# RWKV preparation stage: token mixing and small sums on GpSimd, early hats, and key sums behind the third G product

## The chip, the cores and the metric

One Trainium2 chip (trn2), one of its cores. The metric is the device time of one launch in microseconds. Engines in the profile's names: PE is TensorE (PEld its weight loads), DVE VectorE, ACT ScalarE, POOL GpSimd, SP SyncE, which here only issues DMAs.

## The reference, cut to what matters

A hybrid diffusion block (depth 1, 2048 latent tokens and 256 context tokens, width 1024): a normalised, modulated input goes through one projection into four mixers (gMLP, neighbourhood attention, bidirectional RWKV-7, pooling), which are gated, merged and projected. The edited stage is the part of the RWKV branch that needs no state yet:

```python
zf = centred_shift_mix(z_in, mu)      # z + (0.5 * (prev + next) - z) * mu, 7 tiles of 128 channels
r, k, v, w_lo, a_lo = split(zf)
kk = k * rw_kk;  kk = kk / max(sqrt(sum(kk * kk)), 1e-12)
for d in range(2):                    # forward, backward
    w = -softplus(-(w0[d] + tanh(w_lo) @ w2[d])) - 0.5
    a = sigmoid(a0[d] + a_lo @ a2[d])
    kd = k * (1 + (a - 1) * k_a)
    y[d] = wkv7_scan(r, exp(-exp(w)), kd, v, -kk, kk * a)
    bonus[d] = sum(r * kd * r_k) * v
o = groupnorm(y[0] + y[1]) + bonus[0] + bonus[1]
```

The scan is computed in chunks of 64 tokens. Per chunk this stage makes P and Q (what the chunk does to the state), G (what the state adds to the output) and Y (the part of the output inside the chunk); a later stage chains the states.

## The kernel before, in words

Three stages follow one another, with all engines meeting between them: the front stage (projection), `recurrence_stage` and `late_stages`. Inside the second, `recurrence_local_stage` is edited. It walks 2304 tokens in nine blocks of 256 (`RB`); each block n has two units, (n,0) forward and (n,1) backward. In every unit TensorE does the main work of this unit and, between it, the small products that prepare the next one. `nxt` is the unit prepared: (n,1) during (n,0), (n+1,0) during (n,1).

Each engine has its own instruction stream written out by hand; the order in it is the order of execution. Semaphores count results: `Turns` gives each named result of an engine a number within a unit (`U` numbers per unit), `done` raises the semaphore and `after(engine, unit, name)` waits for it.

TensorE's main work inverts a unit triangular 64x64 matrix per chunk and head in levels v = 1 to 5. Level v: product G{v}, evicted by VectorE with a mask (L1211); product X{v}, evicted by ScalarE (L1334); product Z{v}, evicted by ScalarE. X{v} waits for G{v}'s eviction, G{v+1} for that of X{v}. `beside(v)` is set between G{v} and X{v}: the SK product (v=1), the LoRA product for the decay "tw" and the turned b (2), the LoRA product for the rate "ta" and the turned k (3), the key sums "ks" (4), MV and the norm columns "rnT" (5). `between(v)` is set between Z{v} and G{v+1}: V (3), A (4). After level 5 follow the bonus product, W, the next unit's first scores SB (they wait for the hat b, L1152), the products of G and Y, the first inverse SM, and P and Q.

VectorE in a unit: the five G evictions; behind the first the P and Q of the unit before (`last_products`, L1203, L1204) and the mask product MK (L1220), which TensorE's "tw" group waits for; in (n,1) the seven mixes of block n+1 (L1099) and kk_sq (L1103); behind the third the decay (L1108 to L1113, a scan among them); behind the fourth the Newton steps for the norm (L1119 to L1125, only in (n,1)), kd (L1129) and in (n,0) the two kd_sum steps (L1133, L1134); behind the fifth the hats: kk, R (L1144), kka (L1147), A (L1148), K (L1150), B (L1152). ScalarE evicts, does tanh, the scalings of the seven tiles (L1280), the rates, and the exponentials "EI", "EN" and "tot" (L1311 to L1315), which the hats wait for. GpSimd makes the neighbour sums of a block (L1007), the first Z (L1049), copies R (L1051), resets the identities X0 and MB (L1056, L1064) and copies the LoRA weights of one direction into the buffer used by the products (L1061), once "ta" is done. SP loads z two blocks ahead (`load`, L964) and stores G, Y and the bonus.

Of the kernel before, what the change touches and what calls it, by code (L numbers as in the profile page):

```python
# [21 lines left out]
P = 128  # L22
# [8 lines left out]
CH = 64  # L31
# [800 lines left out]
class Turns:  # L832

    def __init__(self, ctx, nc, name, results, each=None, first=0, leaves_out=((), ())):
# [36 lines left out]
def recurrence_local_stage(nc, t, s, chain):  # L871
# [8 lines left out]
    with ExitStack() as ctx:  # L880
# [29 lines left out]
        lora, lora_of = sb("lora", [P, 2 * P]), sb("lora_both", [P, 2, 2 * P])  # L910
# [7 lines left out]
        U = 64  # L918
        mixes, newton = [f"{j}" for j in (6, 2, 3, 0, 1, 4, 5)], ["nx", "n0"] + [f"n{i}{x}" for i in range(3) for x in "abc"] + ["rx"]
        block_v = [f"mix{j}" for j in mixes] + ["ksq"] + newton + ["kk"]  # L920
        block_a = [f"scaled{j}" for j in mixes] + ["th", "kkr0", "kkr1", "rrk0", "rrk1"]
        prep_v = Turns(ctx, nc, "prep_vector", [f"mix{j}" for j in mixes] + ["ksq", "lw", "L", "Lx", "inc"] + newton
                       + ["kd", "kds", "bt", "kk", "R", "kka", "A", "K", "B", "bonus"], U,
                       leaves_out=(("Lx", "inc", "kds", "bt", "bonus"), block_v))
        prep_a = Turns(ctx, nc, "prep_scalar", [f"scaled{j}" for j in mixes]
                       + ["th", "kkr0", "kkr1", "tw0", "tw1", "rrk0", "rrk1", "ta0", "ta1", "u0", "u1", "EI", "EN", "tot"], U,
                       leaves_out=((), block_a))
        main_v = Turns(ctx, nc, "main_vector", ["G1.", "P0.", "Q0.", "P1.", "Q1.", "MK.", "G2.", "G3.", "G4.", "G5.", "Ya0.", "Gs0.", "Ya1.", "Gs1."],
                       U, first=1, leaves_out=(("Ya0.", "Ya1."), ()))
        main_a = Turns(ctx, nc, "main_scalar", ["X1.", "Z1.", "X2.", "Z2.", "Bt.", "X3.", "Z3.", "Kt.", "V.", "X4.", "Z4.", "At.", "MV.", "Z5.",  # L930
                                                "W0.", "W1.", "Y0.", "Y1."], U, first=1, leaves_out=((), ("V.", "Y0.", "Y1.")))
        main_g = Turns(ctx, nc, "main_pool", ["Z.", "R.", "X0.", "lora.", "MB."], U, first=1)
# [5 lines left out]
        nbr_set, pe_go, dve_go, kept_set, centre_set = (sem(n) for n in ("neighbours_set", "pe_go", "dve_go", "kept_identities_set", "centre_set"))  # L938
        pool_go, lora_set = sem("pool_go"), sem("first_lora_set")
# [18 lines left out]
        def _(sp):  # L958
            def load(n):
                if not first_block(n):  # L960
                    sp.wait_ge(nbr_set, n)
                    prep_a.after(sp, (n - 1, 0), "scaled5")
                c0 = 0 if first_block(n) else n * RB + 1
                sp.dma_start(zin[:], t["zT"][T_RW:T_RG, :, bass.ds(c0, RB + 2)].rearrange("k p t -> p k t")).then_inc(z_in, 16)  # L964

            load(0)
            for d in range(2):
                sp.dma_start(lora_of[0:CH, d, :], t["rw_w2"][0, d, :, :]).then_inc(consts_in, 16)
                sp.dma_start(lora_of[CH:P, d, :], t["rw_a2"][0, d, :, :]).then_inc(consts_in, 16)
# [17 lines left out]
            load(1)  # L987
            sp.wait_ge(rpb_in, 16)
# [6 lines left out]
            turn(NBLK - 1, False)  # L995
            sp.wait_ge(g_stored, 16 * 2 * NBLK)
# [5 lines left out]
        def _(pool):  # L1002
            def neighbours(n):
                pool.wait_ge(z_in, n * 16 + 16)
                if not first_block(n):
                    prep_v.after(pool, (n - 1, 0), "mix5")
                nc.gpsimd.tensor_tensor(nbr[:], zin[:, :, 0:RB], zin[:, :, 2:RB + 2], ALU.add).then_inc(nbr_set, 1)  # L1007

            def prologue():
# [15 lines left out]
                neighbours(0)  # L1025
                for v, b in enumerate(LEVELS):
# [12 lines left out]
                pool.wait_ge(consts_in, 16 * 12)  # L1039
                nc.gpsimd.tensor_copy(lora[:], lora_of[:, 0, :]).then_inc(lora_set, 1)  # L1040
                prep_p.after(pool, (0, 0), "ta")
                nc.gpsimd.tensor_copy(lora[:], lora_of[:, 1, :]).then_inc(main_g.sem, main_g.each)
# [3 lines left out]
            def unit(n, d, nxt):  # L1046
                tiled = lambda a: a.rearrange("p q g m t -> p (q g m) t")
                head_v.after(pool, (n, d), "MB.")
                main_g.done(nc.gpsimd.tensor_tensor(tiled(Z[:]), tiled(MB[:]), eight(lev0[:, d, :]), ALU.mult), d, "Z.")  # L1049
                pool.sem_inc(pool_go, 1)  # L1050
                main_g.done(nc.gpsimd.tensor_copy(Rk[:, d], AR[:, 1]), d, "R.")  # L1051
# [8 lines left out]
                pool.sem_inc(pool_go, 1)  # L1060
# [1997 lines left out]
```

## Time and profile before

| what | value |
|---|---|
| median of 3 runs | 2461.0 us (2460.78 to 2463.07) |
| the profiled execution, own time | 2462.29 us |
| its span | 2460.6 us |
| busy share of the span: PE, DVE, ACT, POOL | 92%, 63%, 41%, 11% |
| the edited stage within the span | about 1262 to 1792 us |
| mean granted TensorE clock | 0.969 |

In the timeline each row is one run of like instructions: start, time from the first start to the last end, engine, line, operation, out<-in, count, and in brackets the idle time of the engine before it and what released it. In the rows by group the time before the bar is busy time and mean duration, behind it idle time and releasers. A window's row gives the busy time and (count) for PE, PEld, DVE, ACT, POOL, then the granted TensorE clock, the DMA share and GB/s.

### The profile page before, as it was taken

What the parts mean: (1) busy time and instruction counts of PE and PEld (TensorE: products, weight loads), DVE (VectorE), ACT (ScalarE), POOL (GpSimd) and SP (SyncE); (2) the same over time, 40 slices, a digit from 0 to 9 for tenths busy, and PEclk for the clock granted to TensorE, in tenths of its full rate; (3) what the DMA queues carried; (4) which work ended last, traced back from release to release, by engine and by line L of the source; (5) the groups of instructions that cost most, each with busy time, mean ns of one, the idle gap of its engine ahead of it and who ended that gap; (6) DMA issues with size and microseconds to landing.
All of it is one profiled execution on the core that took longest, in us unless ns stands there. A gap on an engine that the chain in (4) does not pass through costs nothing. (4 is left out here: it accounts for less than half of the span.)

```text
span 2460.6 us, 66375 instructions
## 1 busy us (share of the span) xinstructions
PE 2263.6 (92%) x26630; PEld 1853.4 (75%) x26630; DVE 1551.8 (63%) x2611; ACT 1009.5 (41%) x1734; POOL 265.3 (11%) x335
## 2 busy tenths in 40 slices
PE   4999999999899999999947899999788799899998
PEld 2788878888688887888836777777657576688887
DVE  5756566666865456665635777777456676856754
ACT  5444234544532123445424555555333666411111
POOL 0000000000000000000031222222124663000000
PEclk7999999999999999999978999999978899999999
DMA  7344333333242333333330111110068523834542
GB/s 240 107 135 125 111 94 111 113 117 102 94 129 93 96 108 97 106 111 119 107 101 25 32 41 32 32 56 17 19 214 305 126 94 95 288 115 171 197 152 88
DMA packets 250306, 277.75 MB, mean 113 GB/s; under 512 B 30683, under 2 KB 174171, under 8 KB 247643
## 3 DMA queue, kind: packets, MB, share of 16 engines
q1 hardware_dynamic: 245306, 266.95, 33.9%
q10 hardware_dynamic: 4576, 8.40, 0.9%
q8 instruction: 70, 1.15, 0.2%
q0 software_dynamic: 320, 0.98, 0.2%
q14 instruction: 34, 0.27, 0.0%
HBM read 184.66 MB, written 91.62 MB: 112 GB/s over the span
## 5 line engine op out<-in xcount | busy, mean ns | idle before, releaser
L715 PE MATMUL proj_ps<-h_hi,w_hi 128*128 128x512 f32 x1656 | 649.5, 392 | 27.6 <-DVE h_lo L465 19.7
L716 PE MATMUL proj_ps<-h_lo,w_hi 128*128 128x512 f32 x1656 | 647.0, 391 | 0.0
L717 PE MATMUL proj_ps<-h_hi,w_lo 128*128 128x512 f32 x1656 | 646.4, 390 | 0.0
L318 ACT CAST w_hi<-w_raw 128x512 fp32r<-128x512 f32 x420 | 255.1, 621 | 694.0 <-PE proj_ps L717 353.2
L715 PEld LDWEIGHTS proj_ps<-h_hi,w_hi 128*128 128x128 f32 x1656 | 312.3, 189 | 98.2 <-issue 26.1
L717 PEld LDWEIGHTS proj_ps<-h_hi,w_lo 128*128 128x128 f32 x1656 | 312.2, 189 | 65.6
L716 PEld LDWEIGHTS proj_ps<-h_lo,w_hi 128*128 128x128 f32 x1656 | 312.4, 189 | 62.9
L482 DVE TENSOR_TENSOR w_lo<-w_raw,w_hi 128x512 fp32r<-128x512 f32 x420 | 283.2, 689 | 44.3 <-ACT w_hi L318 43.7
L498 DVE TENSOR_TENSOR z_slots<-proj_ps,x_rows 128x512 f32<-128x512 f32 x174 | 120.2, 691 | 169.9 <-PE proj_ps L717 167.9
L498 DVE TENSOR_TENSOR x_rows<-proj_ps,x_rows 128x512 f32<-128x512 f32 x116 | 80.1, 691 | 108.9 <-PE proj_ps L717 102.9
L1010 POOL MEMSET rpb_padded<- 60x127 f32 x1 | 0.2, 198 | 1261.3 <-POOLq L89 1261.3
L1211 DVE TENSOR_TENSOR inv_g<-rw_ps,level_masks 128x512 f32<-128x512 f32 x90 | 62.1, 690 | 97.2 <-PE rw_ps L1387 97.1
L2903 PE MATMUL late_ps<-late_lo,mw_hi 128*128 128x512 f32 x252 | 98.0, 389 | 0.0
L1334 ACT COPY inv<-rw_ps 128x512 f32<-128x512 f32 x72 | 42.0, 583 | 125.0 <-PE rw_ps L1387 125.0
L494 DVE COPY x_rows<-proj_ps 128x512 f32<-128x512 f32 x58 | 40.0, 690 | 73.6 <-PE proj_ps L717 73.5
L2492 DVE CUSTOM_DVE_ANT_0 scores<-na_ps,bias_windows 128x768 f32<-128x768 f32 x64 | 61.3, 957 | 34.4 <-issue 25.3
L2448 ACT ACTIVATE late_rows<-scores,softmax_stats 128x768 f32<-128x768 f32 x64 | 60.1, 940 | 52.3 <-DVE softmax_stats L2495 52.3
L2945 PE MATMUL late_ps<-wo_hi,y_hi 128*128 128x512 f32 x208 | 81.3, 391 | 0.0
L2947 PE MATMUL late_ps<-wo_hi,y_lo 128*128 128x512 f32 x208 | 81.0, 389 | 0.0
L2946 PE MATMUL late_ps<-wo_lo,y_hi 128*128 128x512 f32 x208 | 80.9, 389 | 0.0
L332 ACT ACTIVATE z_slots<-z_slots 128x512 f32<-128x512 f32 x128 | 70.6, 621 | 14.1 <-DVE z_slots L498 9.0
L2728 ACT ACTIVATE late_ps<-late_rows 128x1024 f32<-128x1024 f32 x15 | 15.4, 1030 | 125.8 <-DVE late_rows L2818 125.8
(380 smaller groups left out, 4101.4 us busy)
## 6 DMA issues: line engine op xcount, KB each, us to landing
w_raw<-in_w_in SPq DMA_DIRECT2D x240, 256.0 KB, 3.0
scratch_gatesT<-z_slots SPq DMA_DIRECT2D x128, 256.0 KB, 2.7
late_rows<-scratch_gatesT SPq DMA_DIRECT2D x64, 512.0 KB, 4.4
scratch_zT<-z_slots SPq DMA_DIRECT2D x108, 256.0 KB, 2.4
ada<-in_ada_w SPq DMA_DIRECT2D x4, 2048.0 KB, 15.2
late_rows<-scratch_zT SPq DMA_DIRECT2D x4, 2048.0 KB, 12.7
late_rows<-scratch_branchT SPq DMA_DIRECT2D x16, 512.0 KB, 5.3
late_rows<-in_x SPq DMA_DIRECT2D x16, 512.0 KB, 4.9
```

The source lines that it names most:

```text
L318: A.copy(wh[:, i, :, :], raw[:, q, :, :]).then_inc(w_hi, 1)
L332: A.activation(zs[:, q, :], zs[:, q, :], ACT.Sigmoid).then_inc(gated, 1)
L482: V.tensor_tensor(wl[:, i, :, :], raw[:, W_SOURCE[i], :, :], wh[:, i, :, :].bitcast(F32), ALU.subtract).then_inc(w_lo, 1)
L498: V.tensor_tensor(to, ps[:, BANK[n], :], part[:, {1: 0, 3: 0, 4: 2, 5: 0, 6: 1}[n], :], ALU.add).then_inc(ev, 1)
L715: T.matmul(out, wh[:, i, k, :], hi[:, o, k, :], start=(first and k == 0), stop=False, skip_group_check=not first)
L716: T.matmul(out, wh[:, i, k, :], lo[:, o, k, :], start=False, stop=False, skip_group_check=not first)
L717: last = T.matmul(out, wl[:, i, k, :], hi[:, o, k, :], start=False, stop=(k == 3), skip_group_check=not first)
L1211: done(V.tensor_tensor(eights(G[:]), ps[:, 2:4, 0:256].rearrange("p q (k t) -> p q k t", t=CH), mask, ALU.mult), f"G{v}.", *(("P0.", "Q0." ...
L2903: T.matmul(o, hi, b_lo[:, i % 2, k, :], start=False, stop=False)
L2945: T.matmul(o, y_hi[:, k, rows], wo_hi[:, k, cols], start=(k == 0), stop=False)
L2946: T.matmul(o, y_hi[:, k, rows], wo_lo[:, k, cols], start=False, stop=False)
L2947: last = T.matmul(o, y_lo[:, k, rows], wo_hi[:, k, cols], start=False, stop=(k == KT - 1))
```

## The change

Work moves from VectorE and ScalarE to GpSimd, several steps of the next unit's preparation come earlier, and buffers change:

- The mix of a block is made on GpSimd alone, block-wide: neighbour sums, times mu/2, own values times 1 - mu (in place in the loaded tile), then sums "z6", "z23", "z01", "z45". kk_sq, kd_sum and its product with r_rk, the identity added to P, and Y forward plus Y backward go to GpSimd as well. ScalarE copies P and the backward unit's Y out of PSUM for that.
- The LoRA weights of a direction are loaded by SP into the one buffer `lora` for each unit, after "ta"; GpSimd's copy goes. The load of z for block n+2 stands behind this in SP's queue.
- The key sums follow the third G product, and the norm squares (nx) are evicted behind the third G eviction.
- R, K (and kka in the backward case) are made behind the fourth G eviction by `hats_early`, which waits for "tot"; `hats`, behind the fifth, keeps kk, kka of the forward case, B and A, in this order. The exponentials come before the w_in copy in (n,0) and before the X4 copy in (n,1). tanh and the raw keys of the next block are made at the end of (n,0).

The diff, cut to its core (the prologue's counterparts, names of semaphores and buffers are left out):

```diff
 # SP
             def turn(n, more):
                 for d in range(2):
+                    if not (last and d):
+                        prep_p.after(sp, (n + d, 1 - d), "ta")
+                        load_lora(d)
+                    if d == 0 and not first_block(n):
+                        y_out(n - 1)
                     if d and more:
                         load(n + 2)
                     main_v.after(sp, (n, d), "Gs1.")
...
+            def y_out(n):
+                sp.wait_ge(y_added, n + 1)
+                sp.dma_start(t["yT"]..., yst[:]).then_inc(y_stored, 16)
 # GpSimd
+            def scaled_neighbours(n):
+                pool.wait_ge(mix_step, n * 3 + 1)
+                G_.tensor_tensor(nbr[:], nbr[:], per_tile(hmu), ALU.mult).then_inc(mix_step, 1)
+            def scaled_own(n):
+                pool.wait_ge(mix_step, n * 3 + 2)
+                G_.tensor_tensor(own, own, per_tile(omu), ALU.mult).then_inc(mix_step, 1)
+            def mixed_tiles(n, name, j, k):
+                mix_g.done(G_.tensor_tensor(zf[:, j:k, :], nbr[:, j:k, :], own[:, j:k, :], ALU.add), 0, name)
+            def bonus_rows(n):
+                prep_v.after(pool, (n, 1), "kd")
+                keys_g.done(G_.tensor_tensor(kds[:], kd[:, 0], kd[:, 1], ALU.add), 1, "kds")
+                keys_g.after(pool, (n, 1), "kds")
+                prep_a.after(pool, (n, 0), "rrk1")
+                keys_g.done(G_.tensor_tensor(kds[:], kds[:], rrk[:], ALU.mult), 1, "bt")
...
             def unit(n, d, nxt):
                 head_v.after(pool, (n, d), "MB.")
                 main_g.done(... Z ..., d, "Z.")
+                if d and nxt:
+                    key_squares(n + 1)
+                    mixed_tiles(n + 1, "z01", 0, 2)
+                    prep_v.after(pool, (n, 1), "bonus")
+                    mixed_tiles(n + 1, "z45", 4, 6)
                 kept = nc.gpsimd.tensor_copy(Rk[:, d], AR[:, 1])
+                    main_a.after(pool, before, "P.")
+                    main_g.done(add_identity(*before), d, "P.")
+                    if d == 0:
+                        add_y(n - 1)
                 main_p.after(pool, (n, d), "G1.")
                 main_g.done(... X0 ..., d, "X0.")
-                if d == 0 and not (isinstance(n, int) and n == NBLK - 1):
-                    neighbours(n + 1)
-                prep_p.after(pool, nxt, "ta")
-                main_g.done(nc.gpsimd.tensor_copy(lora[:], lora_of[:, d, :]), d, "lora.")
+                if d == 0:
+                    if more:
+                        scaled_own(n + 1)
+                        prep_p.after(pool, nxt, "ta")
+                        mixed_tiles(n + 1, "z6", 6, 7)
+                    bonus_rows(n)
+                    if more:
+                        mixed_tiles(n + 1, "z23", 2, 4)
+                elif not (isinstance(n, int) and n >= NBLK - 2):
+                    neighbours(n + 2)
+                    scaled_neighbours(n + 2)
                 main_p.after(pool, (n, d), "G5.")
                 main_g.done(... MB ..., d, "MB.")
...
 # VectorE
             def last_products(n, d, done):
-                main_p.after(dve, (n, d), "PQ.")
+                main_a.after(dve, (n, d), "P.")
-                    done(V.tensor_tensor(to(Pst), pq[:, :, 0, :, :], eye, ALU.add), f"P{c}.")
...
                     if v == 3 and nxt:
+                        if d:
+                            norm_squares(nxt[0])
                         decay(*nxt)
                     if v == 4 and nxt:
                         if d:
                             norms(nxt[0])
                         rates(*nxt)
-                        if d == 0:
-                            bonus_rows(n)
+                        hats_early(*nxt)
                 if nxt:
                     hats(*nxt)
 # ScalarE, unit
-                if nxt and d:
-                    scaled(nxt[0])
-                    tanh_lo(nxt[0])
                 factor(X[:], "X1.", 4)
...
                 if nxt:
                     key_rates(*nxt)
+                    if d:
+                        exps(*nxt)
+                        bonus_keys(nxt[0])
                 factor(X[:], "X4.", 4)
                 factor(Z[:], "Z4.", 0)
+                if nxt and d == 0:
+                    exps(*nxt)
                 main_p.after(act, (n, d), "A.")
                 own(A.copy(... WI ...), "At.")
-                if nxt:
-                    exps(*nxt)
...
+                for c in range(2):
+                    own(A.copy((yst2 if d else yst)..., ...), f"Y{c}.")
+                if d == 0 and not (isinstance(n, int) and n == NBLK - 1):
+                    tanh_lo(n + 1)
+                    raw_keys(n + 1)
+                main_p.after(act, (n, d), "PQ.")
+                main_g.after(act, (n, d), "P.")
+                own(A.copy(pst[:], ...), "P.")
 # TensorE
                     if v == 2:
-                            main_g.after(pe, u, "lora.", 1)
+                            pe.wait_ge(lora_in, u + U)
                     if v == 3:
                         if more:
                             a_lora(u, -1)
+                            key_sums(u, -1)
                         main_a.after(pe, u, "Bt.")
                         turned(Kh, "K.")
-                    if v == 4 and more:
-                        key_sums(u, -1)
...
-                    if v == 4 and more:
+                    if v == 3 and more:
                         prep_v.after(pe, u, "nx", -1)
...
             def first_scores(u, back):
-                prep_v.after(pe, u, "B", back)
+                prep_v.after(pe, u, "A", back)
```

## Rows read from the trace of the kernel before

**Rows 1.** Windows, one block's units: us, busy PE, PEld, DVE, ACT, POOL, clock, DMA

```profile
1418.27:1443.53 25.26, 23.53 (x871) 20.20 (x871) 17.95 (x30) 14.30 (x31) 7.51 (x6) 1.00 0.06 21
1443.53:1470.35 26.82, 23.80 (x870) 20.33 (x871) 19.95 (x45) 15.17 (x33) 4.77 (x5) 1.00 0.17 54
```

**Rows 2.** Timeline of TensorE in (n,0): start, us, [idle before <- releaser]

```profile
1430.49 0.69 PE L1387 MATMUL rw_ps<-inv,m_b 64*64 64x64 f32 x32
...
1431.11 1.05 PE L1387 MATMUL rw_ps<-heads,kk_sq 128*128 128x2 f32 x8
...
1432.10 0.69 PE L1387 MATMUL rw_ps<-inv_g,inv_t 64*64 64x64 f32 x32
...
1435.27 0.69 PE L1387 MATMUL rw_ps<-inv_t,inv_g 64*64 64x64 f32 x32
...
1436.95 1.10 PE L1387 MATMUL rw_ps<-w_in_rows,inv_t 64*64 64x128 f32 x32
...
1438.92 1.10 PE L1387 MATMUL rw_ps<-a_r_hat,b_hat 64*64 64x128 f32 x32 [0.87 <-DVE b_hat L1152]
...
1439.82 0.44 PE L1387 MATMUL rw_ps<-m_r,w_rows 64*64 64x64 f32 x16
```

**Rows 3.** Timeline of TensorE in (n,1)

```profile
1448.18 0.69 PE L1387 MATMUL rw_ps<-inv,m_b 64*64 64x64 f32 x32 [0.61 <-ACT inv L1334]
...
1458.52 0.69 PE L1387 MATMUL rw_ps<-inv_g,inv_t 64*64 64x64 f32 x32 [0.44 <-DVE kk_norm_inv L1120]
...
1462.06 0.69 PE L1387 MATMUL rw_ps<-inv_t,inv_g 64*64 64x64 f32 x32 [0.31 <-issue]
```

**Rows 4.** Groups by line in the stage: busy us, mean ns | idle before, releaser

```profile
L1099 DVE SCALAR_TENSOR_TENSOR z_mixed<-neighbours,half_mu,z_mixed 128x256 f32<-128x256 f32 x63 | 26.9, 475 | 0.7 <-ACT z_mixed L1280 0.7
```

**Rows 5.** Timeline of ScalarE in (n,0)

```profile
1433.34 0.59 ACT L1334 COPY inv_t<-rw_ps 128x512 f32<-128x512 f32 x1
...
1435.34 0.21 ACT L1315 COPY chunk_decay<-e_padded 128x8 f32 x1
...
1438.12 1.07 ACT L1375 COPY w_rows<-rw_ps 128x512 f32<-128x512 f32 x2 [1.50 <-PE rw_ps L1387]
```

**Rows 6.** Timeline of VectorE in (n,0)

```profile
1432.20 0.69 DVE L1129 TENSOR_TENSOR k_d<-k_rate,z_mixed 128x512 f32<-128x512 f32 x1 [0.26 <-ACT k_rate L1305]
...
1434.41 0.69 DVE L1211 TENSOR_TENSOR inv_g<-rw_ps,level_masks 128x512 f32<-128x512 f32 x1
...
1435.68 0.69 DVE L1144 TENSOR_TENSOR a_r_hat<-z_mixed,e_padded 128x512 f32<-128x512 f32 x1 [0.58 <-ACT chunk_decay L1315]
...
1438.10 0.68 DVE L1152 SCALAR_TENSOR_TENSOR b_hat<-kk_a,e_neg 128x512 f32<-128x512 f32 x1
```

**Rows 7.** Timeline of VectorE in (n,1)

```profile
1453.83 1.23 DVE L1109 TENSOR_TENSOR_SCAN log_run<-scan_keep,log_w 128x512 f32<-128x512 f32 x1
...
1458.31 0.17 DVE L1120 TENSOR_SCALAR kk_norm_inv<-kk_norm_sq 128x8 int32<-128x8 int32 x1
...
1460.33 0.43 DVE L1125 COPY kk_norm_rows<-kk_norm_inv 128x512 f32<-128x512 f32 x1
```

**Rows 8.** Timeline of GpSimd: the prologue, then (n,1)

```profile
1268.64 3.17 POOL L1007 TENSOR_TENSOR neighbours<-z_halo 128x1792 f32<-128x1792 f32 x1 [1.60 <-DMA z_halo<-scratch_zT]
...
1453.87 1.38 POOL L1061 COPY lora<-lora_both 128x256 f32<-128x256 f32 x1 [8.41 <-PE rw_ps L1387]
```

**Rows 9.** Groups of GpSimd by line, the whole kernel: busy us, mean ns

```profile
L1049 POOL TENSOR_TENSOR inv_t<-m_b,level_turned 128x512 f32<-128x512 f32 x18 | 23.0, 1278 | 113.8 <-DVE m_b L1165 113.8
...
L2437 POOL TENSOR_TENSOR wo_rows<-wo_rows,late_rows 128x1024 f32<-128x1024 f32 x8 | 18.7, 2386 | 22.6 <-DMA wo_rows<-in_w_out 22.6
```

**Rows 10.** Timeline of VectorE in the stage's prologue

```profile
1271.25 0.59 DVE L1087 TENSOR_SCALAR one_less_mu<-mu 128x7 f32<-128x7 f32 x1 [5.71 <-DMA rw_params<-in_rw_a]
```

**Rows 11.** Timeline of SP's queue at the stage's end

```profile
1786.38 0.47 SPq L981 DMA_DIRECT2D scratch_yT<-y_stage  x1
```

**Rows 12.** DMA issues: KB each, median us to landing

```profile
z_halo<-scratch_zT SPq DMA_DIRECT2D x9, 903.0 KB, 5.2
```

More of the change, by code:

```diff
@@ L841, in __init__ @@
         for d in range(2):
-            ends = [self.at[r] - 1 for r in self.made[d][1:]] + [self.each + self.at[self.made[1 - d][0]] - 1]
+            if not self.made[d]:
+                self.adds.append({})
+                continue
+            first = self.each + self.at[self.made[1 - d][0]] if self.made[1 - d] else 2 * self.each + self.at[self.made[d][0]]
+            ends = [self.at[r] - 1 for r in self.made[d][1:]] + [first - 1]
             self.adds.append({r: e - self.at[r] + 1 for r, e in zip(self.made[d], ends)})
@@ L925, in recurrence_local_stage @@
[L925 to L929, printed above, removed]
+        U = 32
+        newton = ["nx", "n0"] + [f"n{i}{x}" for i in range(3) for x in "abc"] + ["rx"]
@@ L987, in _ @@
             load(1)
+            prep_p.after(sp, (0, 0), "ta")
+            load_lora(1)
             sp.wait_ge(rpb_in, 16)
@@ L1038, in prologue @@
                     masks.step(pool, nc.gpsimd.tensor_tensor(lev0[:, d, :], lev[:, 1 - d, 0, :], i64[:], ALU.add))
[L1039 to L1042, printed above, removed]
+                neighbours(1)
+                scaled_neighbours(1)
             eight = lambda m: m.rearrange("p (o t) -> p o t", o=1).to_broadcast([P, 8, CH])
@@ L1064, in unit @@
                 main_g.done(nc.gpsimd.tensor_copy(tiled(MB[:]), eight(i64[:, :])), d, "MB.")
-            units(pool, prologue, unit)
+            prologue()
+            unit(0, 0, (0, 1))
+            unit(0, 1, (1, 0))
+            with hinted_loop(nc, pool, 1, NBLK - 2) as n:
+                unit(n, 0, (n, 1))
+                unit(n, 1, (n + 1, 0))
+            unit(NBLK - 2, 0, (NBLK - 2, 1))
+            unit(NBLK - 2, 1, (NBLK - 1, 0))
+            unit(NBLK - 1, 0, (NBLK - 1, 1))
+            unit(NBLK - 1, 1, None)
+            main_a.after(pool, (NBLK - 1, 1), "P.")
+            add_identity(NBLK - 1, 1).then_inc(pool_go, 1)
+            add_y(NBLK - 1)
         N_MASKS = 1 + 8 * len(LEVELS) + 2 * 5 + 2
@@ L1129, in rates, with hats_early @@
                 prep_v.done(V.tensor_tensor(kd[:, d], uu[:], zf[:, 2:4, :], ALU.mult), d, "kd")
-            def bonus_rows(n):
-                prep_v.after(dve, (n, 1), "kd")
-                prep_v.own(dve, (n, 1), V.tensor_tensor(kds[:], kd[:, 0], kd[:, 1], ALU.add), "kds")
-                prep_v.done(V.tensor_tensor(kds[:], kds[:], rrk[:], ALU.mult), 1, "bt")
+            def hats_early(n, d):
+                done = lambda ins, name: prep_v.done(ins, d, name)
+                prep_a.after(dve, (n, d), "tot")
+                if not (first_block(n) and d == 0):
+                    main_g.after(dve, (n, d), "R.", back=1)
+                if d == 0:
+                    mix_g.after(dve, (n, 0), "z01")
+                done(V.tensor_tensor(chunks(AR[:, 1, :, :]), chunks(zf[:, 0:2, :]), padded(d, 1 - d), ALU.mult), "R")
+                prep_v.after(dve, (n, d), "kd")
+                done(V.tensor_tensor(Kh[:], kd[:, d], EN[:], ALU.mult), "K")
+                if d:
+                    done(V.scalar_tensor_tensor(kka[:], aa[:], 1.0, kk[:], ALU.add, ALU.mult), "kka")
             def hats(n, d):
@@ L1182, in prologue @@
                 rates(0, 0)
+                hats_early(0, 0)
                 hats(0, 0)
@@ L1272, in _ @@
             act.wait_ge(consts_set.sem, 8)
[L1274 to L1280 removed]
             def tanh_lo(n):
[L1283 removed]
+                mix_g.after(act, (n, 0), "z6")
                 prep_a.done(A.activation(th[:], zf[0:CH, 6, :], ACT.Tanh), 0, "th")
             def raw_keys(n):
[L1287 removed]
+                mix_g.after(act, (n, 0), "z23")
                 for p in range(2):
@@ L1318, in prologue @@
             def prologue():
-                scaled(0)
                 tanh_lo(0)
@@ L1412, in key_sums @@
             def key_sums(u, back):
-                prep_v.after(pe, u, "ksq", back)
+                mix_g.after(pe, u, "ksq", back)
                 for g in range(2):
```

166 lines of the change are left out of this document (81 added, 85 removed).

## The prediction

> **What bounds the kernel now.** I first split the span by stage. The edited stage prepares the RWKV recurrence, in nine blocks of two units each. The windows of one steady block show 25.26 us for the unit (n,0) and 26.82 for (n,1), 52.08 together. TensorE is busy 23.5 and 23.8 of these at a granted clock of 1.00, VectorE 18.0 and 20.0, GpSimd only 7.5 and 4.8 [rows 1]. So at most some 4.8 us per block, 43 us in all, can be won by taking waits away, and every microsecond by which a product is held up is paid in full. The timelines of TensorE, ScalarE and VectorE in one block show where it waits: 0.87 us for b_hat in each unit [rows 2], 0.61 for a ScalarE copy in (n,1) (it stands behind the tanh) and 0.44 for the first norm step [rows 3]. Elsewhere each eviction is covered by a product set beside it.
>
> **The change part by part.** Times below are those of the shown block, moved.
>
> *Work leaves VectorE and ScalarE.* The seven mixes (26.9 us in nine blocks [rows 4]) go, and ScalarE's seven scalings of the same tiles, with kk_sq, the two kd_sum steps, the identity added to P and the addition of Y. ScalarE gains a copy of P per unit and the Y copies of the backward unit, about 0.6 each like its other copies [rows 5], at the unit's end, where it idles. Of this relief only what stood before a waiting product counts: the mask product MK comes two steps earlier, 0.15 us for TensorE in (n,0); in (n,1) this and the tanh are worth 0.8.
>
> *Key sums.* G4 is issued at 1430.49, the key sums at 1431.11, X4 at 1432.10 [rows 2]. X4 needs G4's eviction: 0.69 product, 0.07, 0.69 VectorE [rows 6], 0.14, together 1.59 us, and 1.61 is there. The key sums (0.99) cost nothing now: they lie in that wait. After G3 there is already a LoRA product and a transpose, so there they are added in full, and behind G4 the wait stays, empty. Cost +0.99 in (n,0), less the 0.15 above: X4 moves to about 1432.9. In (n,1) X4 waited 0.44 more anyway [rows 3]; with the 0.8 won, X4 comes 0.4 earlier than now.
>
> *The early hats.* VectorE's R, K and kka now stand between G4's eviction and G5's, and the first waits for "tot" of ScalarE. In (n,0) ScalarE makes it after the Z4 copy. That copy moves from 1433.34 to about 1434.1. From it to tot were 2.00 us, to 1435.34, with a copy of 0.48 between that now comes after; tot takes 0.21 [rows 5]: it is there at 1435.87. VectorE's hats have a pitch of 0.605 (1435.68 to 1438.10 is four [rows 6]), so G5's eviction starts at 1435.94 + 1.81 = 1437.75, ends at 1438.4, and Z5 is issued at 1438.57, where it was 1435.27 [rows 2]: +3.3 us. (The w_in copy, now behind the exponentials, also holds the norm columns, but only to about 1436.4.) Given back: b_hat is now ready in time. The G/Y products waited for the scores behind b_hat (they start at 1439.82, 4.55 after Z5); now they wait for the copies of W: 1.68 from Z5 to W, 1.10, 0.07, 1.07, 0.15 [rows 2, 5] are 4.07. **(n,0) without any contention: +3.3 - 0.5 = +2.8.**
> In (n,1) the exponentials precede the X4 copy and with the r_rk copies delay it (G5 +0.7). VectorE has ten Newton steps (2.0 us, from 1458.31 to the spread at 1460.33 [rows 7]), the spread, kd, R and K before G5's eviction. They start 0.3 earlier, behind G4's eviction, but R and K come on top: Z5 about 1463.0 where it was 1462.06 [rows 3]; less 0.5: **+0.5**.
>
> *GpSimd.* Without the LoRA copies it keeps about 10 us per block (four small groups per unit) and gets: scaled neighbours, scaled own, the sums of 1792 columns, kk_sq, two kd_sum steps, four identity additions and the Y addition. The nearest rows: 3.17 for 1792 columns where both inputs are of one tensor (1.77 ns per column), 1.28 for 512 with a broadcast (2.5) and 2.39 for 1024 (2.3) where they are two [rows 8, 9]. I take 2.3, as these read two tensors: 4.2 us for each scaling, bounds 3.17 and 4.5. That makes about 29 us of 52: not a bound by itself.
>
> *VectorE against GpSimd.* What counts is when they meet. GpSimd's LoRA copy of 256 columns at 1453.87 took 1.38 us, more than twice a 512-column copy: VectorE's scan of two SBUF inputs ran 1453.83 to 1455.06, and the copy ended 0.2 after it [rows 7, 8]. The other way round: VectorE's 7-column one_less_mu started at 1271.25, took 0.59 and ended at 1271.84, 0.03 after GpSimd's neighbours (1268.64 + 3.17) [rows 8, 10]. So each waits for the other's whole instruction. Nowhere before does a VectorE step with two SBUF inputs start inside a long GpSimd one; I take it that it waits like the 7-column one; the other bound is that it doesn't wait at all.
> The Trainium skill (SBUF — State Buffer, "SBUF: two separate sides") states this as a rule: the pair of ports is locked for the whole instruction, also against VectorE operations with two SBUF inputs. By that rule the sum is the first one below, without it the second.
> (n,0): bt ends at about 1436.4 (kd, 0.69 from 1432.20 [rows 6], comes 0.9 later with the key rates, then two steps of 1.2), 0.5 after VectorE could start R; then z23 (1.2) and the identity copy (0.6) can slip in between R, K and kka. Z5 +0.5 to +2.5 more, I take 1.5: **+4.3**.
> (n,1): the load of z for block n+2 was issued at the unit's start; now it stands in SP's queue behind the wait for "ta" and two LoRA loads. The LoRA copy at 1453.87 waited for this same ta [rows 8]; it comes 0.9 earlier, plus three issues of 0.5 (like 0.47 [rows 11]) and 5.2 to landing [rows 12]: 1459.7. Then GpSimd adds (3.17) and scales (4.2) without a pause but for a semaphore, to about 1467.3: just where VectorE does the last Newton steps, the spread, kd, R and K. It gets one or two small steps in between; then kd, R, K (1.8) and possibly the identity copy, so G5's eviction ends at about 1470.0 and Z5 is issued at 1470.2, +8.2; less 0.5: **+7.7** (bounds +5.5 and +8.7). Seven blocks have such a load; the eighth such unit costs +0.5.
>
> *Ends of the stage.* Prologue: the LoRA product no longer waits for the masks, but GpSimd mixes block 0 before building them and runs block 1's neighbours before its first Z; -2 to +2, taken as 0, as G1 still needs the masks. End: Y was stored from 1786.38 [rows 11]; now it follows the P copy, two identity additions and the sum, issued near 1790.6: +4.5 at the barrier. LoRA loads of two 64 KB have a unit's time before their use: 0. The waits for y_added and y_stored lie a unit behind: 0.
>
> **Sum:** 9 x 4.3 + 7 x 7.7 + 0.5 + 4.5 = +98 us. The profiled execution took 2462.3 us (span 2460.6), 1.3 above the median of 2461.0; 2462.3 + 98 - 1.3 = 2559; rounded down for the smaller bounds, **2556 us**.
>
> **Rivals.**
> 1. *The engines don't exclude each other* in this pairing: 9 x 2.8 + 8 x 0.5 + 4.5 = +34, 2495 us. For it: the one VectorE wait on record is of a small one-input step. Against: the scan shows the opposite direction for just this form.
> 2. *The lock holds, but loads land beside other work* (z earlier or later than the Newton steps, VectorE's run not broken): half of (n,1)'s price, 9 x 3.5 + 7 x 3.5 + 5 = +61, 2522 us.
> 3. *Faster:* the relief of VectorE reaches TensorE. Place: G5's eviction. If tot and the three hats were done before G5's product ends, all waits of [rows 2, 3] go (0.87 twice, 0.44, 0.61, about 0.7 of small ones: 3.5) and only the key sums (1.4 per block) stay: 9 x -2.1 + 4.5 = -15, 2446 us. It decides where tot is 2.6 us earlier in (n,0) than I work out and GpSimd's long steps meet no VectorE step. Against: ScalarE's order is written out, Z4's copy before the exponentials.
> 4. *Nothing measurable:* gains and losses cancel; only by accident.
> The clock stays at 1.00 (2.4 GHz) in this stretch [rows 1]; longer idle times of TensorE might lower it, which the upper end allows for.
>
> **How the numbers follow.** Chances: forecast 0.5, rival 1 0.2, rival 2 0.15, faster 0.12, nothing 0.03. The forecast's own range is 2525 to 2590. The range over the cases, 2482 to 2590, leaves out the faster and the equal case and a little above. A difference of over 0.2% (5 us) can be told from none here; slower 0.85, same 0.03, faster 0.12.
>
> **What would show it.** Right: in (n,0) VectorE waits for tot before R, and G5's eviction follows kka; X4 is released by G4's eviction with no product between; in (n,1) GpSimd runs two long instructions back to back some 16 us into the unit while a VectorE step that took 0.2 or 0.68 us lasts several; the block period is near 64 us. No VectorE duration stretched and a period of 55 makes rival 1 right; GpSimd's long steps elsewhere, rival 2; a period under 52, rival 3.

## The result: slower by 4.7%, and the profile after

| | before | after |
|---|---|---|
| median of 4 runs each, us | 2462.0 (2460.8 to 2466.1) | 2579.9 (2572.6 to 2580.5) |
| ratio | | 1.047, 95% interval 1.045 to 1.049 |
| profiled execution, span, us | 2460.6 | 2577.9 |
| first G1 of the stage, us | 1310.41 | 1312.49 |
| last G1 of the stage, us | 1759.73 | 1878.32 |
| busy share PE, DVE, ACT, POOL | 92%, 63%, 41%, 11% | 89%, 60%, 39%, 16% |
| mean granted TensorE clock | 0.969 | 0.949 |

Predicted were 2556 us and a range of 2482 to 2590. All of the loss lies in the stage: from its first to its last G1 there are 565.8 us instead of 449.3, 116.5 more, and the spans differ by 117.3. The windows of one steady block, (n,0) and then (n,1), answer to [rows 1] (columns as there):

```profile
1448.34:1479.74 31.40, 24.91 (x871) 20.69 (x871) 17.45 (x24) 14.63 (x32) 14.47 (x12) 0.95 0.06 21
1479.74:1515.61 35.87, 26.78 (x871) 22.23 (x871) 22.34 (x34) 13.74 (x30) 14.62 (x12) 0.86 0.14 44
```

(n,0) is 6.1 us longer and (n,1) 9.1. GpSimd is busy 29 us of 67 and bounds nothing by itself, but TensorE's busy time rose by 1.4 and 3.0 us for the same number of products. The granted clock (0.95 and 0.86, the third number from the right) was 1.00 in both units before.

**(n,0).** TensorE, to hold against [rows 2] (start, us, and idle time before it with its releaser):

```profile
1461.39 0.69 PE L1455 MATMUL rw_ps<-inv,m_b 64*64 64x64 f32 x32
1462.94 0.69 PE L1455 MATMUL rw_ps<-inv_g,inv_t 64*64 64x64 f32 x32 [0.86 <-issue]
...
1466.63 0.63 PE L1494 MATMUL rw_ps<-ident,kk_norm_rows 128*128 128x128 f32 x4 [1.04 <-ACT w_in_rows L1430]
1470.57 1.13 PE L1455 MATMUL rw_ps<-inv_t,inv_g 64*64 64x64 f32 x32 [3.31 <-DVE inv_g L1295]
1471.63 2.06 PE L1455 MATMUL rw_ps<-kd_sum,heads 128*128 128x512 f32 x2
1473.62 1.10 PE L1455 MATMUL rw_ps<-w_in_rows,inv_t 64*64 64x128 f32 x32
...
1476.01 0.46 PE L1455 MATMUL rw_ps<-m_r,w_rows 64*64 64x64 f32 x16 [0.41 <-ACT w_rows L1436]
```

X4 (the row at 1462.94) has nothing between it and G4 and waits 0.86 us: the cover of the key sums is gone. Its row names "issue", but what came last was G4's eviction, which ended 0.10 us before it (1462.15 + 0.69, first row below). Z5 waits 3.31 us for G5's eviction. The wait for b_hat of [rows 2] is gone, as the scores follow the W product at once. VectorE and GpSimd in the same stretch show why the eviction is late:

```profile
1462.15 0.69 DVE L1295 TENSOR_TENSOR inv_g<-rw_ps,level_masks 128x512 f32<-128x512 f32 x1 [1.29 <-PE rw_ps L1455]
...
1466.03 1.20 DVE L1223 TENSOR_TENSOR a_r_hat<-z_mixed,e_padded 128x512 f32<-128x512 f32 x1 [2.23 <-ACT chunk_decay L1381]
1467.15 1.66 DVE L1225 TENSOR_TENSOR k_hat<-k_d,e_neg 128x512 f32<-128x512 f32 x1
1468.73 1.09 DVE L1227 SCALAR_TENSOR_TENSOR kk_a<-a_tanh,kk_unit 128x512 f32<-128x512 f32 x1
1469.75 0.68 DVE L1295 TENSOR_TENSOR inv_g<-rw_ps,level_masks 128x512 f32<-128x512 f32 x1
```
```profile
1465.41 1.27 POOL L1046 TENSOR_TENSOR kd_sum<-kd_sum,r_rk 128x512 f32<-128x512 f32 x1 [0.23 <-ACT e_padded L1377]
1466.63 1.63 POOL L1035 TENSOR_TENSOR z_mixed<-neighbours,z_halo 128x512 f32<-128x512 f32 x1
1468.21 1.07 POOL L1144 COPY m_b<-ident 128x512 f32<-128x512 f32 x1
```

R waits 2.23 us for tot and stands ahead of the eviction. Then the engines take turns: R, K and kka take 1.20, 1.66 and 1.09 us where one took 0.69 before [rows 6], each with a GpSimd step that ends inside it.

**(n,1).** The queue of SP, then GpSimd, VectorE and TensorE:

```profile
1489.22 0.48 SPq L969 DMA_DIRECT2D lora<-in_rw_w  x1
1489.74 0.60 SPq L970 DMA_DIRECT2D lora<-in_rw_a  x1
1490.64 0.41 SPq L966 DMA_DIRECT2D z_halo<-scratch_zT  x1
```
```profile
1495.86 3.17 POOL L1024 TENSOR_TENSOR neighbours<-z_halo 128x1792 f32<-128x1792 f32 x1 [10.45 <-DMA z_halo<-scratch_zT]
1499.11 3.19 POOL L1028 TENSOR_TENSOR neighbours<-neighbours,half_mu 128x1792 f32<-128x1792 f32 x1
```
```profile
1495.68 0.17 DVE L1207 TENSOR_TENSOR kk_norm_step<-kk_norm_inv,kk_norm_sq 128x8 f32<-128x8 f32 x1
1495.88 3.18 DVE L1208 SCALAR_TENSOR_TENSOR kk_norm_step<-kk_norm_step,kk_norm_inv 128x8 f32<-128x8 f32 x1
1499.09 0.17 DVE L1209 SCALAR_TENSOR_TENSOR kk_norm_inv<-kk_norm_step,kk_norm_inv 128x8 f32<-128x8 f32 x1
1499.29 3.29 DVE L1210 COPY kk_norm_rows<-kk_norm_inv 128x512 f32<-128x512 f32 x1
1502.50 1.09 DVE L1214 TENSOR_TENSOR k_d<-k_rate,z_mixed 128x512 f32<-128x512 f32 x1
...
1504.72 0.68 DVE L1295 TENSOR_TENSOR inv_g<-rw_ps,level_masks 128x512 f32<-128x512 f32 x1
```
```profile
1502.73 1.09 PE L1494 MATMUL rw_ps<-ident,kk_norm_rows 128*128 128x128 f32 x4 [4.99 <-DVE kk_norm_rows L1210]
1505.55 1.13 PE L1455 MATMUL rw_ps<-inv_t,inv_g 64*64 64x64 f32 x32 [1.73 <-DVE inv_g L1295]
1506.61 2.07 PE L1455 MATMUL rw_ps<-kd_sum,heads 128*128 128x512 f32 x2
1508.62 1.99 PE L1455 MATMUL rw_ps<-w_in_rows,inv_t 64*64 64x128 f32 x32
```

The z load lands 16.1 us into the unit. GpSimd's two long steps start at once, and an 8-column Newton step of VectorE that began 0.02 us after the first took 3.18 us instead of 0.17 and ended 0.03 after it; the spread, begun in the second, took 3.29 instead of 0.43 [rows 7]. TensorE waits 4.99 + 1.73 us.

**The clock.** The products behind both waits are slow: the bonus product took 2.06 and 2.07 us, against 1.12 in experiment 7 below, where the clock stays up. Windows of the two units, from Z5 to the start of the next unit's scores in (n,0), and to their end in (n,1):

```profile
1470.57:1474.55 3.98, 3.98 (x67) 2.37 (x70) 1.59 (x3) 0.59 (x1) 0.00 (x0) 0.63 0.00 0
1505.55:1511.89 6.34, 6.23 (x99) 4.40 (x99) 2.43 (x4) 1.66 (x3) 0.00 (x0) 0.56 0.00 0
```

The granted clock is 0.63 and 0.56 on average here, so for most of both windows it was at 0.5, the lower of its two levels (1.2 of 2.4 GHz). In (n,1) it was already at 0.50 from 1502.73 to 1505.55, between the two waits: there the norm columns took 1.09 us.

### The profile page after: what moved, and what is told of

It is laid out like the page before. It is cut to its first block and busy times, and to the rows that moved or that the text cites. A ratio compares the mean times of both kernels' runs of the same rounds, so it can differ in the third digit from the quotient of the medians.

```text
span 2577.9 us, 66380 instructions
## 1 busy us (share of the span) xinstructions
PE 2297.9 (89%) x26630; PEld 1874.2 (73%) x26630; DVE 1559.6 (60%) x2467; ACT 1000.7 (39%) x1707; POOL 417.1 (16%) x442
## 5 line engine op out<-in xcount | busy, mean ns | idle before, releaser
L715 PE MATMUL proj_ps<-h_hi,w_hi 128*128 128x512 f32 x1656 | 650.0, 392 | 28.6 <-DVE h_lo L465 20.9
L1455 PE MATMUL rw_ps<-inv_t,inv_g 64*64 64x64 f32 x2880 | 67.8, 234 | 40.5 <-DVE inv_g L1295 40.5
L1399 ACT COPY inv_t<-rw_ps 128x512 f32<-128x512 f32 x90 | 53.1, 590 | 101.6 <-PE rw_ps L1455 101.6
L1455 PEld LDWEIGHTS rw_ps<-inv_t,inv_g 64*64 64x64 f32 x2880 | 58.2, 148 | 45.2 <-issue 45.2
```

The costliest lines, as they stand in the source:

```text
L715: T.matmul(out, wh[:, i, k, :], hi[:, o, k, :], start=(first and k == 0), stop=False, skip_group_check=not first)
L1399: own(A.copy(to.rearrange("p q g m t -> p q (g m t)"), ps[:, bank:bank + 2, 0:256]), name)
L1455: mm = lambda o, l, r, start=True, stop=True: T.matmul(o, l, r, start=start, stop=stop)
```

## The experiments

A ratio is to runs of the kernel before on the same chip; "units" are distances from G1 to G1 in steady blocks. Before: (n,0) 25.3, (n,1) 26.8, together 52.1. After: 31.4 to 32.4 and 34.9 to 35.9, together 66.5 to 68.0.

**1. After, with the z load ahead of the LoRA loads.**

```diff
+                    if d and more:
+                        load(n + 2)
                     if not (last and d):
                         prep_p.after(sp, (n + d, 1 - d), "ta")
                         load_lora(d)
...
-                    if d and more:
-                        load(n + 2)
```

> The changed kernel with the load of z for block n+2 put ahead of the wait for ta and of the two LoRA loads on SP. Theory (the two long GpSimd instructions shut VectorE out during the Newton steps): they then run about 8 to 16 us into the unit (n,1), where VectorE mostly evicts PSUM; the unit falls from 35.9 us to 29 to 31, and TensorE's clock no longer drops behind it; in all 35 to 48 us less, 2532 to 2545. Rival (VectorE's own chain in (n,1) is simply too long, or the clock drops by itself): under 5 us less, above 2575.

Measured: 2537.3 us, 1.029 (1.027 to 1.031). (n,1) fell to 29.8, (n,0) stayed at 31.7. GpSimd starts 8.3 us into the unit instead of 16.1, and the same two GpSimd steps now meet other VectorE steps, the Newton steps none:

```profile
1479.39 1.20 DVE L1190 TENSOR_SCALAR log_w<-log_w 128x512 f32<-128x512 f32 x1
1480.70 4.01 DVE L1191 TENSOR_TENSOR_SCAN log_run<-scan_keep,log_w 128x512 f32<-128x512 f32 x1
1484.83 0.69 DVE L1295 TENSOR_TENSOR inv_g<-rw_ps,level_masks 128x512 f32<-128x512 f32 x1
```

The scan took 4.01 us instead of 1.23 [rows 7], and X4 waits 2.9 us for the eviction behind it. So the load's place costs 43 us, and GpSimd's steps hold VectorE where they fall now too, only at a cheaper place.

**2. After, with R, K and kka behind the fifth eviction.** The call of `hats_early` moves to where `hats` is called.

```diff
                         rates(*nxt)
-                        hats_early(*nxt)
                 if nxt:
+                    hats_early(*nxt)
                     hats(*nxt)
```

> The changed kernel with the early hats (R, K, kka) called behind the fifth G eviction, as before the change. Theory (R to kka hold the fifth eviction and with it Z5): the unit (n,0) falls from 31.4 to 27 to 28.5 us; in (n,1) only R and K move, while the long GpSimd instructions still hold kd, so it falls by 1 to 2.5; in all 40 to 50 us less, 2530 to 2540. Rival (order on VectorE does not matter, GpSimd's instructions set the pace): under 10 us less.

Measured: 2533.4 us, 1.028 (1.026 to 1.030); (n,0) 27.6 at a clock of 1.00, (n,1) 33.8 at 0.90. The early hats cost 4 to 5 us in (n,0), the clock's fall behind their wait included. In (n,1) two Newton steps took 3.04 and 3.03 us: the collision is untouched.

**3. After, with the key sums behind G4.** The call and the first norm step go back to where they were.

```diff
                             a_lora(u, -1)
-                            key_sums(u, -1)
...
+                    if v == 4 and more:
+                        key_sums(u, -1)
```

> The changed kernel with the key sums and the norm squares back behind the fourth G product. Theory (behind G3 they are added in full, behind G4 they fill a wait that is there anyway): 0.9 us less in (n,0), 0.5 to 0.9 in (n,1), 12 to 16 us less in all, about 2566. Rival (their place is free): within 3 us of 2580.

Measured: 2569.1 us, 1.041 (1.039 to 1.043); two units about 66. The direction is right; the size is known to some microseconds only, as the runs spread from 2561 to 2577.

**4. Before, with the key sums behind G3 and nothing else** (the same edit the other way, on the kernel before).

> The kernel before with this one part of the change: key sums and norm squares behind the third G product. Theory: +1.0 us in (n,0), +0.5 in (n,1), 12 to 15 us more, about 2475. Rival: they come earlier and free the 0.44 us wait for the norm, so no loss or a gain of up to 4 us (2458 to 2462).

Measured: 2476.9 us, 1.0046 (1.0031 to 1.0061). (n,0) 26.1, (n,1) 27.15: +0.85 and +0.33, where the prediction has 0.99, and in (n,1) 0.99 less the 0.44 that X4 waited anyway. X4 waits 0.86 in both units.
That is five of the eight (n,1) units. The other three took 28.6 us, at a clock of 0.94. In the one that starts at 1448.04, the clock is 0.54 from 1460 to 1463 us, and the V product behind Z3 took 1.62 us instead of 1.16. No wait of TensorE above 0.86 us stands in that unit, and none above 0.61 ahead of the fall: here the clock fell without a long stall.

**5. Before, with R, K and kka ahead of the fifth eviction.** Of the rest of the change it has only what belongs to this order: `hats` makes B ahead of A, and the scores wait for A.

```diff
                         if d == 0:
                             bonus_rows(n)
+                        hats_early(*nxt)
                 if nxt:
                     hats(*nxt)
```

> The kernel before with one part of the change alone: VectorE makes R hat, K hat and (in the backward unit) kka ahead of the eviction of G5. Mixing stays on VectorE, key sums behind G4, z load where it was. Theory (the hats hold G5's eviction until tot and three steps of 0.605 us are done, with no contention from GpSimd): (n,0) longer by 1.5 to 2.5 us, (n,1) by 0 to 0.5, so some 54.5 to 55 for two units instead of 52.1, about 2482 to 2490 us in all, and Z5 waits some 3 us for the eviction in (n,0). Rival (the order of the hats costs nothing by itself, it is GpSimd that makes the wait): within 3 us of before, about 2462 to 2465.

Measured: 2508.9 us, 1.018 (1.017 to 1.020): more than expected. The windows of four units of this kernel, two (n,0) and two (n,1), say where the rest comes from:

```profile
1398.66:1428.56 29.90, 25.39 (x870) 21.16 (x871) 20.16 (x45) 15.12 (x33) 4.76 (x5) 0.94 0.16 48
...
1428.56:1456.43 27.87, 23.59 (x871) 20.23 (x871) 17.95 (x30) 14.39 (x31) 7.50 (x6) 1.00 0.06 19
1486.21:1516.28 30.07, 26.27 (x870) 22.12 (x871) 17.97 (x30) 14.32 (x31) 7.52 (x6) 0.89 0.05 17
...
1516.28:1544.55 28.27, 23.90 (x870) 20.30 (x871) 20.18 (x45) 15.19 (x33) 4.77 (x5) 1.00 0.17 51
```

At a clock of 1.00 the order alone costs +2.6 us in (n,0) (27.87) and +1.45 in (n,1) (28.27). The same unit of the same program takes 1.6 to 2.2 us more when the clock fell in it (29.90, 30.07), with TensorE's busy time up by 1.5 and 2.7. That happened in about half of the units, behind a wait of 2.3 to 2.9 us for the eviction; the same wait is also there in units where the clock held, so it does not follow from the wait's length alone. (TensorE's rows name "issue" for this wait; in (1,0) the eviction ended at 1390.70 and Z5 followed at 1390.80.)

**6. After with all three undone.** The handing to GpSimd stays, and with it the exponentials' new place and A behind B.

> The kernel after with three parts undone together: z load ahead of the LoRA loads in SP's queue, the hats behind G5's eviction, the key sums behind G4. What is left is the handing of mixing and sums to GpSimd. Theory (the three costs are separate, and what remains of the loss is GpSimd's long steps meeting VectorE elsewhere): (n,0) about 26.5 to 27, (n,1) 28 to 29, 55 for two units, 2485 to 2500 us, still slower than before. Rival (once the order is right, VectorE's relief of three mixes per unit pays): two units under 52, below 2460 us. Second rival (the parts overlap, so undoing the third gives nothing more): like the better of the two single undoings less 30 us, above 2503 us.

Measured: 2494.5 us, 1.012 (1.011 to 1.014). (n,0) 26.74, (n,1) 29.4 to 29.8. VectorE in (n,1), and GpSimd's two steps:

```profile
1465.62 0.69 DVE L1295 TENSOR_TENSOR inv_g<-rw_ps,level_masks 128x512 f32<-128x512 f32 x1 [3.07 <-PE rw_ps L1454]
1466.22 2.74 DVE L1190 TENSOR_SCALAR log_w<-log_w 128x512 f32<-128x512 f32 x1
1469.07 4.01 DVE L1191 TENSOR_TENSOR_SCAN log_run<-scan_keep,log_w 128x512 f32<-128x512 f32 x1
```
```profile
1465.51 3.17 POOL L1024 TENSOR_TENSOR neighbours<-z_halo 128x1792 f32<-128x1792 f32 x1 [2.75 <-DMA z_halo<-scratch_zT]
1468.76 3.24 POOL L1028 TENSOR_TENSOR neighbours<-neighbours,half_mu 128x1792 f32<-128x1792 f32 x1
```

The eviction, which reads PSUM and one mask, ran its 0.69 us inside GpSimd's step. The two steps behind it, SBUF only, did not: 2.74 and 4.01 us instead of 0.42 and 1.22. X4 waits 3.2 us for what VectorE does behind them (2.6 in the first block), and in all seven of these units the clock falls (0.94 over the unit). In the (n,1) units of experiment 1, with a wait of 2.6 to 3.0 us at the same place, it stayed at 1.00. The one (n,1) unit without a load took 26.31, half a microsecond under before: the only place where relieving VectorE of the mixes shows as a gain. (n,0) is 1.5 over: R, K and kka still take 1.04, 1.67 and 1.09 us there, and TensorE waits 1.2 for A hat behind them. What is left of the change loses 30 us, the clock's part in it included.

**7. The kernel of experiment 1 with idle time filled.** Four products from constants ahead of the wait for G5's eviction; the result is read by nobody.

```diff
+                    if v == 5:
+                        for _ in range(4):
+                            mm(ps[:, 0, 0:256], J[:], tri[:].rearrange("p a b c -> p (a b c)"))
                     main_v.after(pe, u, f"G{v}.")
```

> The kernel of a1 (after with the early z load, 2537 us) with four products of 128x256 columns from constants set between the norm columns and Z5, about 2.1 us of TensorE work whose result nobody reads. They lie in the wait for G5's eviction, 3.31 us in (n,0) and 1.68 us in (n,1). Theory (TensorE's clock falls to its lower level because it idled in (n,0), and the bonus product and W behind the wait then take 2.02 and 1.83 us instead of 1.13 and 1.10): with the wait filled the clock stays at 1.00 there, (n,0) is 1.3 to 1.7 us shorter, (n,1) 0.4 longer where the products overshoot, 2525 to 2531 us. Rival (the clock falls for another reason, or its fall costs nothing in time): the two products as slow as before, 2537 to 2542 us.

Measured: 2524.3 us, 1.024 (1.023 to 1.026), 13 us less with more work for TensorE. TensorE in (n,0), first in experiment 1, then filled:

```profile
1459.31 0.69 PE L1455 MATMUL rw_ps<-inv_t,inv_g 64*64 64x64 f32 x32 [3.31 <-DVE inv_g L1295]
1459.93 2.02 PE L1455 MATMUL rw_ps<-kd_sum,heads 128*128 128x512 f32 x2
1461.88 1.83 PE L1455 MATMUL rw_ps<-w_in_rows,inv_t 64*64 64x128 f32 x32
```
```profile
1457.26 1.89 PE L1455 MATMUL rw_ps<-chunk_masks,heads 128*128 128x256 f32 x8
1460.74 0.69 PE L1455 MATMUL rw_ps<-inv_t,inv_g 64*64 64x64 f32 x32 [1.59 <-DVE inv_g L1295]
1461.36 1.12 PE L1455 MATMUL rw_ps<-kd_sum,heads 128*128 128x512 f32 x2
1462.42 1.10 PE L1455 MATMUL rw_ps<-w_in_rows,inv_t 64*64 64x128 f32 x32
```

(n,0) went from 31.7 to 30.0 at a clock of 1.00, and the two products run at full speed; so they do in all seven units from (1,0) to (7,0), none of which kept the clock in experiment 1. (n,1) is 29.4 to 31.1: there the clock now falls in six of the seven units with a load, around X4's wait; in experiment 1 it fell in none of them, with that wait at 2.6 to 3.0 us. So the time behind the stall in (n,0) is a cost of its own, and TensorE's idling there is what brings it on; where else the clock falls, these runs do not say.

**8. After, with GpSimd's two long steps writing only.** This kernel leaves out the neighbours of blocks 2 to 8; all other work stands where it was.

```diff
-                    neighbours(n + 2)
-                    scaled_neighbours(n + 2)
+                    for k in range(2):
+...
+                        G_.tensor_tensor(nbr[:, :, 0:1], zin[:, :, 0:1], zin[:, :, 2:3], ALU.add)
+                        G_.memset(nbr[:, :, 1:RB], 0.5).then_inc(mix_step, 1)
```

> The kernel after, where GpSimd's two long steps in (n,1) are replaced, in the loop and in the units around it, by a 7-column addition (it carries the wait) and a fill of the same 1785 columns with a constant. So the neighbours of blocks 2 to 8 are not computed; everything else stands, the place of the steps too. Theory (GpSimd shuts VectorE out because both read SBUF at the same pair of ports, so it counts what the two instructions read): the fills, which read nothing, either do not hold VectorE at all or only for their own, shorter, time; then (n,1) falls from 35.9 to about 27.7, what the unit without a load took in after, and the total to about 2520 us (7 blocks of 8). Rival (any GpSimd instruction shuts VectorE out for its whole length): Newton steps of VectorE last as long as a fill, and (n,1) is longer than 27.7 by the two fills' durations, 2525 to 2550 us according to their length.

Measured: 2533.9 us, 1.028 (1.027 to 1.030). GpSimd, then VectorE:

```profile
1483.65 1.59 POOL L1147 MEMSET neighbours<- 128x1785 f32 x1
...
1485.52 1.58 POOL L1147 MEMSET neighbours<- 128x1785 f32 x1
```
```profile
1483.77 0.17 DVE L1214 SCALAR_TENSOR_TENSOR kk_norm_step<-kk_norm_step,kk_norm_inv 128x8 f32<-128x8 f32 x1
1483.97 0.17 DVE L1215 SCALAR_TENSOR_TENSOR kk_norm_inv<-kk_norm_step,kk_norm_inv 128x8 f32<-128x8 f32 x1
1484.17 1.35 DVE L1216 COPY kk_norm_rows<-kk_norm_inv 128x512 f32<-128x512 f32 x1
...
1486.04 0.68 DVE L1229 TENSOR_TENSOR a_r_hat<-z_mixed,e_padded 128x512 f32<-128x512 f32 x1
```

Neither theory holds as put. The steps with two SBUF inputs run through both fills at their usual 0.17 and 0.68 us; only the spread, a copy with one input, was held (1.35 instead of 0.43). (n,1) took 28.2 and 28.4 in the two units where the clock stayed at 1.00, near the 27.7 expected, and 29.9 to 30.0 in the five where it fell. The total missed its 2520 by 14 us; those falls, 1.6 us each, are 8 of them.
The Trainium skill (SBUF — State Buffer, "SBUF: two separate sides") says that VectorE steps with two SBUF inputs are excluded only against a GpSimd step that reads SBUF, and those in a two-port mode against any. It names a copy of fp32 within SBUF as such a step, which the spread is. The trace agrees on both counts: 0.17 and 0.68 us beside the fill, 1.35 for the copy.

**9. Before, with K hat behind B hat.** A version to beat both.

```diff
                 prep_v.after(dve, (n, d), "kka")
                 done(V.scalar_tensor_tensor(Bh[:], kka[:], 0.5, EN[:], ALU.mult, ALU.mult), "B")
+                prep_v.after(dve, (n, d), "kd")
+                done(V.tensor_tensor(Kh[:], kd[:, d], EN[:], ALU.mult), "K")
```

> The kernel before with VectorE's K hat moved behind B hat, nothing else. B hat is what TensorE waits for (0.87 us in each unit), K hat is needed only behind G1 of the next unit. Theory (that wait ends last in the unit): each of 18 units shorter by one VectorE step of about 0.5 to 0.6 us, 8 to 10 us in all, 2452 to 2454 us, and the wait for b_hat is 0.3 us. Rival (the G/Y products wait for the copies of W right behind, and cover the wait): 2461 to 2463 us.

Measured: 2456.4 us, 0.9963 (0.9949 to 0.9976). Units 24.79 and 26.33, each 0.48 shorter. The wait for b_hat is 0.27 us where it was 0.87 [rows 2].

**10. The kernel of 9 with ScalarE's tanh behind the X1 copy.**

```diff
                     scaled(nxt[0])
-                    tanh_lo(nxt[0])
                 factor(X[:], "X1.", 4)
+                if nxt and d:
+                    tanh_lo(nxt[0])
```

> The kernel of b3 (before with K hat last, 2456 us, units 24.79 and 26.33) with ScalarE's tanh of the next block set behind the copy of X1 instead of ahead of it in (n,1). Theory (G2 waits 0.61 us there for the copy, which stands behind a tanh that waits for VectorE's mix of tile 6): (n,1) shorter by 0.3 to 0.6 us, eight times, so 2451 to 2454 us, ratio to before about 0.994. Rival (the LoRA product behind G2 then waits for the tanh, or the copy of Z1 comes late): (n,1) 26.2 to 26.4, 2455 to 2458 us.

Measured: 2456.8 us, 0.9960 (0.9944 to 0.9975). (n,1) is 26.06, 0.27 shorter: the wait of 0.61 for the X1 copy is gone, and 0.47 for the mask product MK took its place ahead of the LoRA product. Eight times 0.27 is 2.2 us, which the runs cannot tell from experiment 9. Both beat the kernel before.

## Why the prediction was right, and which terms were off

**What held.** The sign, the place and both mechanisms: in (n,0) VectorE waits for tot ahead of R with G5's eviction behind kka; X4 has nothing to cover its wait; in (n,1) GpSimd's long steps run back to back 16 us into the unit and a step of 0.17 us lasts 3.2. Only the block period, forecast near 64 us, was 66.5 to 68. Rival 1 (no exclusion) fell with these rows. Rival 2 (the load lands beside other work) was made true by experiment 1, which gave 2537 us and not the 2522 of its price: even there the steps met the scan. The faster rival fell by experiment 6: VectorE's relief shows as 0.5 us in the one (n,1) unit that GpSimd's long steps don't disturb.

**Term by term**, for the steady block shown:

| term | predicted | measured |
|---|---|---|
| (n,0): Z5 later in the unit | +4.8 | +5.2 (22.23 instead of 17.00 behind G1) |
| (n,1): Z5 later in the unit | +8.2 | +7.3 (25.81 instead of 18.53) |
| b_hat given back, each unit | -0.5 | -0.5 at a clock of 1.00 (7.79 from Z5 to the next G1 in the (n,1) unit without a load, 8.29 before) |
| from Z5 to the next G1, (n,0) | 7.8 | 9.2 |
| from Z5 to the next G1, (n,1) | 7.8 | 10.1 |
| unit (n,0) | +4.3 | +6.1 |
| unit (n,1) | +7.7 | +9.1 |
| (n,1) unit without a load | +0.5 | +0.9 (27.73) |
| key sums alone (n,0), (n,1) | +0.99, +0.55 | +0.85, +0.33 |
| early hats alone (n,0), (n,1) | within +2.8, within +0.5 | +2.6, +1.45 at full clock |
| prologue | 0 | +0.5 (first G1 2.1 later, the stage begun 1.6 later) |
| stage end (last G1 to first load of the next stage) | +4.5 | +3.6 (35.88 instead of 32.27) |

**The term that was mis-sized is the clock.** The prediction put it at 1.00 in the sum and left its fall to "the upper end allows for". It falls with both long waits, and from Z5 on costs 1.4 us in (n,0) and 2.3 in (n,1) of the block shown: 9 x 1.4 + 7 x 2.3 = 29 us, nearly a third of the sum of 98. (Blocks differ: the excess over 7.8 us is 1.4 to 2.3 in either unit, 27.7 us over the fifteen units up to (7,0).) At a clock of 1.00 that stretch took the 7.8 us forecast. That this is the clock, experiment 5 shows: up to 2.2 us between two units of the same code. That idling brings it on in (n,0), experiment 7 shows: 1.7 us won by filling the wait. It is not the only way to the lower level, as three units of experiment 4 show. The other errors partly cancel: (n,0)'s stall was 0.4 larger (+4 us), (n,1)'s 0.9 smaller (-6) because the scaling with a broadcast ran at 3.19 us like the sum of neighbours, not at 4.2 (its rate was taken from 1024-column steps of two tensors), the end 1 us cheaper (its Y store, 1786.38 and 1790.6 in the prediction, makes +4.2 and not the +4.5 entered), and the work behind the stage ran 5 us shorter in this execution. In all 98 + 29 + 4 - 6 - 1 - 5 = 119 against 117.3.

A small mis-reading: the early hats in (n,1) were put at 0.5 and cost 1.45 alone. The prediction credited a head start of 0.3 to 0.8 us that the kernel of experiment 5, which keeps the mixes and scalings, does not have; the unit without a load in the kernel after, 0.9 longer instead of 0.5, has it.

**The parts don't add up to a line.** Undoing each alone gives back 43 (load), 46 (hats) and 11 us (key sums), each the difference of two medians; together 100. All three undone gave 85 us (2579.9 to 2494.5), and 30 stay. The early load moved GpSimd's pair of long steps to the scan, where in experiment 6 they still stretch two VectorE steps by 5 us in all. How much of the missing 15 us is this and how much the clock was not separated.

## What to carry to other kernels

Before a step is handed to GpSimd, ask which VectorE steps run when its input lands. With two SBUF inputs a step waits for the whole GpSimd instruction that reads SBUF, be it 8 columns wide; so did the fp32 steps of 7 and 512 columns with one SBUF input that we saw. The eviction, which reads PSUM and one SBUF operand, passed. Reading SBUF alone is not what decides: in the late stage of the kernel before, a reciprocal of 2 columns (1979.12, 0.16 us) ran at its usual length in the middle of a GpSimd sum of 2061 columns (1976.75, 3.62 us). A step put ahead of an eviction costs what it waits for, not its own length. And a stall of TensorE of some microseconds can have a second price: look at the granted clock of the products behind it, in our case 1.4 to 2.3 us on top.

## What the runs showed of the hardware that was not expected

- The clock's fall is not the same in every unit: in experiment 5 waits of 2.3 and 2.9 us for the same eviction were followed by the lower level in about half of the units, with both outcomes at each place. In experiment 4 it fell in three of eight (n,1) units with no wait of TensorE above 0.61 us in that unit before it, 1.5 us each.
- More work made the kernel faster: four unread products per unit, 1.9 us of TensorE time, took 13 us off the kernel of experiment 1.
- A GpSimd multiply of 1792 columns with a broadcast operand took 3.19 us, the same as a sum of two full operands (3.17); a constant fill of 1785 columns took 1.59.
- GpSimd's fill let VectorE's two-input steps through but held its copy, from 0.43 to 1.35 us.
